# Wide and narrow expert blocks in one loop instead of two loops in a row

## The reference

```python
def moe_ffn(h, router_w, router_bias, w_gate, w_up, w_down, ws_gate, ws_up, ws_down):
    affinity = jax.nn.sigmoid((h @ router_w).astype(f32))
    _, idx = lax.top_k(affinity + router_bias.astype(f32), TOP_K)
    ...
    def expert_block(acc, blk):
        tok, g, e = blk
        y = swiglu(h_ext[tok], w_gate[e], w_up[e], w_down[e])
        return acc.at[tok].add(y * g[:, None]), None
    ...
    return acc[:n_tok] + swiglu(h, ws_gate, ws_up, ws_down)
```

## Time and profile before

| | us |
|---|---|
| median of 3 runs | 3177.21 |
| lowest, highest | 3157.06, 3179.2 |
| the profiled execution | 3183.83 |
| its span, first to last instruction | 3181.7 |
| PE busy in it | 2369.7 |
| mean granted clock of PE (share of 2.4 GHz) | 0.859 |

### The profile page before, as it was taken

How to read it: one execution, slowest core, us unless ns; L and a number is a source line. 1 busy time by engine, 2 the same in 40 slices (tenths; PEclk the granted TensorE clock), 3 DMA queues, 4 the chain that set the end, 5 groups by cost and what they waited for, 6 DMA issues and landing times. The chain is left out here.

```text
span 3181.7 us, 37237 instructions
## 1 busy us (share of the span) xinstructions
PE 2369.7 (74%) x10582; PEld 1275.4 (40%) x10583; DVE 986.4 (31%) x2087; ACT 570.7 (18%) x890; POOL 562.9 (18%) x468
## 2 busy tenths in 40 slices
PE   6896999568587888888887705339965987777772
PEld 1443544344333444444444405336433444444441
DVE  4761235663322111111222245862231111111113
ACT  1122133340211111111111103021021111111110
POOL 2530000000001111111232230400002112222222
PEclk9998999788797898998999956557987988889996
DMA  8675110100415877878999855414036777999995
GB/s 263 243 279 202 52 53 0 66 1 0 195 65 209 279 251 262 283 259 287 395 386 378 319 194 144 106 56 145 1 145 223 259 251 270 396 366 383 377 377 177
DMA packets 183239, 683.82 MB, mean 215 GB/s; under 512 B 34091, under 2 KB 36395, under 8 KB 144795
## 3 DMA queue, kind: packets, MB, share of 16 engines
q1 hardware_dynamic: 136042, 581.86, 49.0%
q0 software_dynamic: 38784, 71.13, 9.4%
q10 hardware_dynamic: 8336, 29.82, 2.3%
HBM read 628.15 MB, written 94.65 MB: 227 GB/s over the span
## 5 line engine op out<-in xcount | busy, mean ns | idle before, releaser
L1372 PE MATMUL pGU_m<-wgu_m,xT_m 128*64 128x256 f32 x2816 | 381.8, 432 | 153.5 <-DMA wgu_m<-in_exp_w_up 153.4
L1361 PE MATMUL pGU_m<-wgu_m,xT_m 128*128 128x512 f32 x800 | 401.9, 661 | 86.6 <-DMA wgu_m<-in_exp_w_up 86.6
L1372 PEld LDWEIGHTS pGU_m<-wgu_m,xT_m 128*64 128x64 f32 x2816 | 223.6, 156 | 346.0 <-DMA wgu_m<-in_exp_w_up 222.4
L1361 PEld LDWEIGHTS pGU_m<-wgu_m,xT_m 128*128 128x128 f32 x800 | 168.4, 214 | 315.1 <-issue 208.9
L1395 PE MATMUL pY_m<-wd_m,hidT_m 128*128 128x512 f32 x400 | 188.3, 614 | 0.1
L1176 POOL DMA_INDIRECT xgn_m<-moe_h,idxn_m x96 | 99.8, 1040 | 496.1 <-DVE idxn_m L1295 474.4
L1416 PE MATMUL pY_m<-wd_m,hidT_m 128*64 128x512 f32 x704 | 173.2, 611 | 4.0
L1828 PE MATMUL acc_p<-w_p,cT_p 128*2 128x512 f32 x384 | 167.9, 596 | 0.0
L1316 DVE COPY hidT_m<-pHT_m 128x128 f32<-128x128 f32 x88 | 25.6, 291 | 435.7 <-PE pHT_m L1404 435.7
L1196 POOL DMA_INDIRECT moe_acc<-yn_m,idxn_m x88 | 140.0, 1591 | 108.8 <-ACT yn_m L1255 99.6
L1231 ACT ACTIVATE xT_m<-pT_m 128x1024 f32<-128x1024 f32 x54 | 55.2, 1023 | 532.4 <-PE pT_m L1347 532.4
(11 more groups left out here) (370 smaller groups left out, 3236.8 us busy)
## 6 DMA issues: line engine op xcount, KB each, us to landing
wgu_m<-in_exp_w_gate SPq DMA_DIRECT2D x138, 1024.0 KB, 10.2
wgu_m<-in_exp_w_up SPq DMA_DIRECT2D x138, 1024.0 KB, 16.6
wd_m<-in_exp_w_down SPq DMA_DIRECT2D x138, 1024.0 KB, 13.1
w_p<-in_mod_w SPq DMA_DIRECT2D x24, 2048.0 KB, 8.4
acc_c<-moe_acc SPq DMA_DIRECT2D x30, 512.0 KB, 10.5
W_a<-in_ar_w_in SPq DMA_DIRECT2D x5, 2048.0 KB, 8.1
moe_acc<-zero_r ACTq DMA_DIRECT2D x20, 512.0 KB, 16.7
s_w<-Wt_p ACTq DMA_DIRECT2D x8, 1152.0 KB, 9.7
```

The lines of the kernel that those rows point to most:

```text
L1361: last = pe.matmul(pGU[b % 2][:], xT[b % 2][:, k, :], wgu[b % WIDE_RING][:, :, k, :], start=(k == 0), stop=(k == KD - 1))
L1372: last = pe.matmul(pGU[b % 2][H * side:H * side + H, 0, :].rearrange("p (j n) -> p j n", j=2), narrow_xT[b % 2][:, k % 4, H * (k // 4):H * ...
```

## The change

Wide and narrow blocks are taken in one loop of max(trips) trips (12 in layer 0, 11 in layer 1, the counts of the table being smaller). Slot number i holds wide block i and narrow block i. Every engine does its steps for both kinds in a fixed order, each step in an If of its own on the count of its kind. Each kind has its own one-hot marks, transposed rows, hidden values, weight slots (still two and three) and PSUM banks; pHT and pI now share a bank, so PE waits for DVE's reading (idx_done) at the end of each rest. The next block's gate and up are no longer taken ahead of this one's rest: the other kind's gate and up stand there. Wide rows are transposed and copied out in two halves. Wide blocks add to accumulator 0 alone, each add waiting for the one before it (yw_added); narrow ones add to 1 and 2 in turn, with two result buffers for three. SP loads gate and up of both kinds first and then down of both. Marks are made five blocks ahead.

```diff
-        def items(eng, n, trips, body):
-            with eng.Fori(0, trips) as q:
+        def trips(eng, n_wide, n_narrow, steps):
+            with eng.Fori(0, TRIPS) as q:
                 for b in range(UNROLL):
-                    with eng.If(n > q * UNROLL + b):
-                        body(q * UNROLL + b, q, b)
+                    i = q * UNROLL + b
+                    for kind, step in steps:
+                        with eng.If((n_narrow if kind else n_wide) > i):
+                            step(i, q, b)
...
-            items(sp, count(sp, 0), WIDE_TRIPS, lambda i, q, b: load(0, i, q, b))
-            items(sp, count(sp, 1), NARROW_TRIPS, lambda i, q, b: load(1, i, q, b))
+            trips(sp, count(sp, 0), count(sp, 1),
+                  ((0, lambda i, q, b: gate_up(0, i, b)), (1, lambda i, q, b: gate_up(1, i, b)),
+                   (0, lambda i, q, b: down(0, i, b)), (1, lambda i, q, b: down(1, i, b))))
...
             def wide(i, q, b):
                 pool.wait_ge(W['idx_done'], i + AHEAD + 1)
-                pool.wait_ge(W['xT_mm'], i + 2)
+                pool.wait_ge(W['xT_mm'], i * 2 + 4)
                 gather_wide((b + AHEAD) % UNROLL)
                 pool.wait_ge(W['y_done'], i + 2)
+                pool.wait_ge(yw_added, i * 16 + 32)
                 pool.sem_inc(W['pool_go'], 1)
-                pool.indirect_dma_start(accs[b % 2], bass.IndirectOffsetOnAxis(idx[0][b][:].bitcast(U32), 0),
+                pool.indirect_dma_start(accs[0], bass.IndirectOffsetOnAxis(idx[0][b][:].bitcast(U32), 0),
                                         y_w[b % 2][:], None, bounds_check=last_row, oob_is_err=False,
-                                        compute_op=ALU.add).then_inc(y_added[b % 2], 16)
+                                        compute_op=ALU.add).then_inc(yw_added, 16)
...
-            def narrow(i, q, b):
-                with pe.If(n_narrow > q * UNROLL + (b + 1)):
-                    up_narrow((b + 1) % UNROLL, i + 2, q * (32 * UNROLL // NARROW_RING) + 32 * ((b + 1) // NARROW_RING + 1), i + 1)
+            def rest_narrow(i, q, b):
                 pe.wait_ge(N['hid_done'], i + 2)
...
+                pe.wait_ge(N['idx_done'], i + AHEAD + 1)
...
-            items(pe, n_wide, WIDE_TRIPS, wide)
-            pe.wait_ge(W['xT_done'], n_wide + 2)
...
-            items(pe, n_narrow, NARROW_TRIPS, narrow)
+            trips(pe, n_wide, n_narrow, ((0, up_wide), (1, up_narrow), (0, rest_wide), (1, rest_narrow)))
```

More of the change, by code:

```diff
@@ L1121, in moe_loop @@
         d_loaded = [[sem(f"d_loaded{s}{b}") for b in range(r)] for s, r in (("w", WIDE_RING), ("n", NARROW_RING))]
+        yw_added = sem("yw_added")
+        yn_added = [sem(f"yn_added{b}") for b in range(2)]
         block = ctx.enter_context(nc.Block())
@@ L1212, in _ @@
             pool.wait_ge(W['idx_done'], 4)
[L1213 removed]
+            pool.wait_ge(W['xT_mm'], 2)
             gather_wide(3)
[L1215 to L1216 removed]
             pool.wait_ge(N['idx_done'], 4)
@@ L1219, in _ @@
             gather_narrow(3)
[L1220 to L1223, removed]
+            nw, nn = count(pool, 0), count(pool, 1)
+            trips(pool, nw, nn, ((0, wide), (1, narrow)))
+            pool.wait_ge(yw_added, nw * 16 + 32)
+            for k in range(2):
+                pool.wait_ge(yn_added[k], (nn + (1 - k)) // 2 * 16 + 16)
             for b in range(3):
@@ L1260, in _ @@
             for b in range(2):
[L1261 to L1265, removed]
+                for half in range(2):
+                    act.wait_ge(W['xT_mm'], 2 * b + half + 1)
+                    evac_wide(b, half)
                 act.wait_ge(N['xT_mm'], b + 1)
                 evac_narrow(b)
-            items(act, count(act, 1), NARROW_TRIPS, narrow)
+            trips(act, count(act, 0), count(act, 1),
+                  ((0, silu_wide), (1, silu_narrow), (0, rest_wide), (1, rest_narrow)))
         @block.vector
@@ L1328, in _ @@
                 tokens(1, i, i)
-            nw = count(dve, 0)
-            items(dve, nw, WIDE_TRIPS, wide)
-            items(dve, count(dve, 1), NARROW_TRIPS, narrow)
+                mark_narrow(i + 1)
+            trips(dve, count(dve, 0), count(dve, 1),
+                  ((0, gated_wide), (1, gated_narrow), (0, rest_wide), (1, rest_narrow)))
         @block.tensor
@@ L1339, in pick, with rows_wide @@
                 for t in range(NT):
-                    last = pe.matmul(pI[:, 0:5], onehot[:, t, :], pick_rhs[:, t, bass.ds(e, 1), :]
+                    last = pe.matmul(pI[:, kind, 0:5], onehot[kind][:, t, :], pick_rhs[:, t, bass.ds(e, 1), :]
                                      .rearrange("p e c -> p (e c)"), start=(t == 0), stop=(t == NT - 1))
                 last.then_inc(S[kind]['idx_mm'], 1)
-            def rows_wide(b):
+            def rows_wide(b, half):
                 rows = xg_w[b % 3][:].rearrange("p (a c k) -> p a k c", a=2, k=KD // 2)
-                for k in range(KD):
-                    last = pe.transpose(pT[:, k * P:(k + 1) * P], rows[:, k // 4, k % 4, :], ident[:])
+                for k in range(4):
+                    last = pe.transpose(pT_w[:, k * P:(k + 1) * P], rows[:, half, k, :], ident[:])
                 last.then_inc(W['xT_mm'], 1)
```

239 lines of the change are left out of this document (115 added, 124 removed).

## The result

The changed kernel takes 3209.48 us (median of 5 runs, 3194.96 to 3217.56) and the kernel before 3177.21. The ratio is 1.0105, with a 95% interval of 1.0065 to 1.0145. The forecast was 3015 in 2970 to 3110, so it is wrong in sign and by 194 us. The profiled spans are 3212.1 and 3181.7 us: +30.4.

The account below looks back on a forecast made before the run. DMA was to bound the merged loop, a pair costing 21.5 us (21.0 plus 0.5 for PE). Loops -113 and -76, work ahead +4, empty slots +22: -163, from 3183.8 to 3021 profiled, median 3015 us, range 2970 to 3110.

Parts of the forecast that it names:

- The waits added, one by one ... nothing: Block loops: added waits for hidden values, indices, half-row transposes and wide adds would be covered by other work, costing nothing.
- PE ... 20.1 us: PE's busy time for one wide plus one narrow block, half-clock parts included, against 21.0 us for DMA.
- 8.6 us, still under 9.1: Narrow blocks once wide ones are used up: PE 7.1 + 1.5 = 8.6 us, DMA still the bound at 9.1.
- PE becomes the bound: Rival, paired loop: clock drops more often or chains show, pair 23.1 us, +74, total 3089 us; chance 0.14.
- the DMA-bound start: Start of the merged loop: two pairs' loads already in, third asked for 7.5 us on; 8 us in the sum.
- DMA's 21.0 us per pair: DMA's need for one wide (11.8 us) plus one narrow block (9.2 us), taken from the old loops.
- The empty slots: Loop slots passed over without a block: 1.2 us each, +20 us in layer 0 and +2 in layer 1.
- The body too long for the code store: Rival: merged loop outgrows engines' code store, one wait for code per empty trip, up to +83 us, 3098; chance 0.08.
- The chain of wide adds: Rival: wide adds to one accumulator, each after the last lands, set the pair: 27.6 us, +281, 3296; chance 0.07.

## Why the prediction was wrong, point by point

- **Failed: "The waits added, one by one ... nothing", and with it "PE ... 20.1 us".** Of the waits that it named, hidden values (hid_done) and indices (idx_done), none ends idle time of PE in the pairs of layer 0, so for them "nothing" was right. It did not name hidT_done, though the change says that pHT and pI share a bank, and it did not ask what stands behind a wait in the sequencer: it took PE's price of a pair from rows of an order in which the pick's load stands behind no such wait. PE's price is 23.4 us, 21.3 busy and 2.1 idle. The load behind the wait costs 23.4 - 20.3 = 3.1 us of a pair in layer 0, half of it as half clock.
- **That 20.3 us with the load ahead is near the 20.1 is luck.** The 20.1 had half-clock parts in it and the 20.3 has none (clock 1.00). At full clock the prediction had 17.9. Of the 2.4 us between, 1.1 are the two longer picks (0.85 and 0.80 for 0.29) and 0.5 the gaps that are left.
- **Failed in size: narrow blocks alone, "8.6 us, still under 9.1".** They take 10.7. Part of it is the same cause: with the loads ahead they take 290 / (1519 / 49) = 9.35, and 7.7 away from the changes of trip. The stops for code, which the prediction had only as a rival, are in both. Where the clock was 1.00, 8.6 us was met, but not by the sum 7.1 + 1.5: it is made of a gap of 0.8 us for the hidden values, one of 0.8 at the pick, and no half-clock parts.
- **The rival "PE becomes the bound" had the bound and nearly the pair (23.1), but not the reason and not the total (3089).** It added two bare chains of hidden values, 2 x 1.5 us. No such chain shows in the pairs; the 3.1 us come from the load and the clock, so the 23.1 is luck. In a loop that PE bounds, all 34 pairs of layer 0 cost the full price; its sum took over the DMA-bound start, where the first two cost 8 us. 34 x 23.4 + 4 x 10.0 (the last narrow blocks of layer 0) is 836, the measured 836.4. The 97 us missed are 32 x 1.9 = 61 for the pairs, 2 x 23.4 - 8 = 39 for the first two, and -3 for the end. In layer 1 it is 14 x 0.4 = 6, 36 for the first two and 34 x 1.6 - 7 = 47 for the narrow blocks: 89 of 92.
- **DMA's 21.0 us per pair** was too high by 1.1 (19.9 measured), and hid nothing, as DMA was not the bound.
- **The empty slots: the tail of layer 0 was met (39.8 for 38.7), the price of a slot was not.** Passing over five empty trips takes 28.4 us away there, 28.4 / 30 = 0.95 for a slot and not 1.2, and 11.4 us stay for the last four slots and what follows. That the two errors cancel is luck. In layer 1 the tail is 26.0 for 16; passing over two empty trips takes 14.2 us away, 1.2 for a slot. DVE's fetches may be the difference; that was not tried by itself.
- **The body too long for the code store**: half right at most. Fetches came, by q14 and DVE's stops; no other queue of instructions moved anything in 2820 to 3140. But they come in layer 1 alone, and in each trip that does work, not just in the empty ones, and whether the length is the reason is open.
- **The chain of wide adds** never got near. The transfer's time from issue to landing, shortest, median and longest in the whole run, against a median of 11.9:

```profile
DMA to landing us min/median/max: 6.1/9.6/11.8
```

## What to carry to other kernels

A wait can cost what is behind it, not only how late it is satisfied: when a change puts a wait ahead of register loads on an engine, move these ahead of the wait (here one line per step, 5.7% of the time). Price an engine from rows in which its instructions stand in the new order, and where none exist, give the term a range that includes a bare register load per wait. And before two loops are merged to fill a queue, count the slots: three in place of two filled it as well.

## What the hardware showed that I had not expected

- A register load behind a wait takes 0.65 us on PE (two in place of one: 1.73 for 1.09 us and 1.61 for 0.95). Behind the wait the six matmuls of a pick take 0.80 to 0.85 us instead of 0.29, with the load ahead of it or not.
- Gaps of about 1 us on PE, two in a pair of 23.4 us, came with a granted clock of 0.94, gaps of 1.7 us with 0.90, and gaps of 0.2 to 0.3 us with 1.00; between the last and the first of these the half clock cost as much as the gaps (1.5 and 1.6 us of a pair).
- Code was fetched again in each trip in one layer and not in the other, with the same loop body on DVE, and DVE stopped for 4.6 to 6.1 us at a time.
